# State-space rounds of a hybrid encoder block: carried products in five PSUM places, transposes in three, and the first round's transposes and updates inside its last two projections

## The chip, the core and the metric

The kernel runs on one core of a Trainium2 chip. TensorE (PE in the profile) multiplies matrices and writes PSUM, VectorE (DVE) and ScalarE (ACT) read PSUM and work on SBUF, GpSimd (POOL) works on SBUF alone, and SyncE (SP) issues the loads of the weights. PSUM has eight banks, each of 512 fp32 numbers a partition. The metric is the device time of one execution in microseconds; smaller is better.

## What is computed

One encoder block (feed-forward, mixer, feed-forward, norm) runs over 16 meta tokens, a prompt of 256 and a sample of 512 tokens, 784 columns together, with a width of 1024. The mixer has two branches; the change is in the first one, a bidirectional state-space scan (SSD) with 16 heads in 4 groups of 4. It is computed in chunks of 128 tokens: two of the prompt, four of the sample. The reference does this for each direction:

```python
def ssd_chunked(x, dt, A, Bm, Cm):
    ...
    CB = jnp.einsum('bctgn,bcsgn->bctsg', Cc, Bc)
    y_diag = jnp.einsum('bctsg,bctsgh,bcsghp->bctghp', CB, Lm, xdt)
    decay_to_end = jnp.exp(acs[:, :, -1:] - acs)
    states = jnp.einsum('bcsgn,bcsgh,bcsghp->bcghpn', Bc, decay_to_end, xdt)
    chunk_decay = jnp.exp(acs[:, :, -1])

    def step(h, inp):
        st, dec = inp
        return dec[..., None, None] * h + st, h
    ...
    y_off = jnp.einsum('bctgn,bcghpn,bctgh->bctghp', Cc, prev, jnp.exp(acs))
    return (y_diag + y_off).reshape(b, T, H, P)
```

## The kernel before

**Projections.** Every weight is split into a high part `whi` (ScalarE) and a low part `wlo` (in this stage by VectorE, helper `low`, L1844), and a projection of 128 output columns is a `job`: for each of 8 slices `t` of the width six matmuls (three products, two column halves) that add up in one of two PSUM slots, `slot[0]` and `slot[1]`, of two banks each. This is a `t` step; a job has 48 matmuls, all on L514. The other four banks are `aux[0]` to `aux[3]`, which the profile names by the tile `aux`.

**A round.** There are four rounds, one for each group of heads (`GROUPS`). A round has six jobs: 0 and 1 for x, 2 for B, 3 for C, 4 and 5 for the gate z. For jobs 0 to 3 ScalarE copies the slot to `ci` (`ssd_read`), VectorE convolves it (`convolve`, L1915 and L1917) and ScalarE applies SiLU and writes `co` (L1249, semaphore `co_ok`). Around the jobs, TensorE does this for the round:

- `ssd_turn`, L738: 8 groups of three transposes (two groups of 16 meta tokens, then the six chunks) into `aux[n % 2]`. ScalarE copies each to `xbt` (L1274, `tr_ok`). Group n waits for the copy of group n - 2.
- `ssd_updates`, L753: ten products for the chunks' states. GpSimd makes the operands `xw` first (L2331), six of them in `co`; VectorE copies the results to `prev` or adds them to the decayed state before (L1940, L1944, L1946, semaphore `up_ok`).
- `ssd_carried`: six products of C and B (L765, `CB` of the reference, in `aux[2]` and `aux[3]`), once all states are there, and then for each chunk c the product of C and the carried state (L774, `y_off` of the reference) into `aux[c % 2]`, 256 columns for each of one or two directions. VectorE multiplies each by its decay and writes it to `prev` (L1953, `off_ok`). Chunk c waits for VectorE to be done with chunk c - 2.
- `ssd_step(k)`, five times: decay products (L791), exponentials (ScalarE, L1290) and outputs (L801, L804), whose gates VectorE applies (`gates`, L1989).

The trace shows each fp32 matmul of L753, L765 and L774 as two entries, so ten instructions of L774 are 20 entries. A transpose is one entry.

**Order.** Every engine has its instructions in an order written out by hand, and waits for semaphores in it; nothing is scheduled at run time. The first round stands ahead of a loop (`Fori`) of three passes. Each pass has jobs 1 to 5 of the next group N between steps 0 to 4 of the group G, then updates and carried products of N, then job 0 of the group behind it. On VectorE a pass has at its end `ssd_updates(N)`, `weighted(G)` (L2003 to L2011), `decays(0, N)` (L1978), one `low`, and `ssd_carried(N)`. In the first round it is `ssd_updates`, `decays(0)`, `low`, `ssd_carried`. GpSimd's products `xdt` (L2339) follow its `xw`.

Ahead of the loop TensorE has this, with the job ahead of `ssd_carried` finished before the first update begins:

```python
            pe.wait_ge(dt_all, 1)
            ssd_turn(first)
            ssd_job(5, first)
            ssd_updates(first)
            ssd_carried(first)
            ssd_job(0, (1, None))
```

## Time and profile before

| | us |
|---|---|
| median of 3 runs | 2342.83 (2342.05 to 2344.07) |
| the profiled execution | 2344.32 |
| its span in the trace | 2342.8 |
| TensorE busy with matmuls | 2263.5 (97%) |
| VectorE busy | 1445.8 (62%) |
| ScalarE busy | 1025.9 (44%) |
| GpSimd busy | 365.4 (16%) |

The profile shows one execution. A busy TensorE there means that a matmul is in flight; a wait shows as idle time in square brackets, with the instruction that ended it. TensorE's clock has two levels, 1.2 and 2.4 GHz; a granted clock of 1.00 is the upper one, 0.50 the lower. The state-space rounds lie between 593 and 977 us: the first round to 660, the three passes of the loop from there to about 747, 833 and 918.

### The profile page before, as it was taken

What the parts mean: (1) busy time and instruction counts of PE and PEld (TensorE: products, weight loads), DVE (VectorE), ACT (ScalarE), POOL (GpSimd) and SP (SyncE); (2) the same over time, 40 slices, a digit from 0 to 9 for tenths busy, and PEclk for the clock granted to TensorE, in tenths of its full rate; (3) what the DMA queues carried; (4) which work ended last, traced back from release to release, by engine and by line L of the source; (5) the groups of instructions that cost most, each with busy time, mean ns of one, the idle gap of its engine ahead of it and who ended that gap; (6) DMA issues with size and microseconds to landing.
All of it is one profiled execution on the core that took longest, in us unless ns stands there. A gap on an engine that the chain in (4) does not pass through costs nothing.

```text
span 2342.8 us, 36390 instructions
## 1 busy us (share of the span) xinstructions
PE 2263.5 (97%) x13148; PEld 2017.3 (86%) x13148; DVE 1445.8 (62%) x2345; ACT 1025.9 (44%) x1659; POOL 365.4 (16%) x256
## 2 busy tenths in 40 slices
PE   8999999998999999999999999999999999999997
PEld 7899999997877777888888888888888899899996
DVE  7667677677788888413444444442237667677677
ACT  6334243244464664523555566644125333243344
POOL 2000000000101201134323333322333100000000
PEclk9999999998999999999999999999999999999998
DMA  3221221223111111132111111111332132221211
GB/s 118 65 73 55 72 72 54 72 57 105 46 37 37 36 36 39 52 97 75 46 37 45 45 45 45 36 37 46 103 121 74 56 86 56 66 78 54 72 54 72
DMA packets 252273, 144.65 MB, mean 62 GB/s; under 512 B 5712, under 2 KB 248576, under 8 KB 252176
## 3 DMA queue, kind: packets, MB, share of 16 engines
q1 hardware_dynamic: 249072, 130.63, 20.0%
q0 software_dynamic: 2336, 12.58, 1.5%
q8 instruction: 62, 1.02, 0.2%
q14 instruction: 35, 0.29, 0.0%
q10 hardware_dynamic: 768, 0.13, 0.0%
HBM read 133.89 MB, written 9.44 MB: 61 GB/s over the span
## 4 chain that ended last, share of the span: by engine, by line
PE 78%; DVE 8%; issue 7%; ACT 5%; POOL 1%; DMA 0%; ACTq 0%; DVEq 0%; POOLq 0%
PE slot L514 31%; PE aux L545 23%; PE slot L594 14%; PE aux L913 2%; PE aux L804 1%; POOL wlo L2269 1%; PE aux L791 1%; PE aux L881 1%; PE aux L906 1%; PE aux L894 1%; PE slot L681 1%; ACT whi L985 1%; PE aux L774 1%; DVE ca L1917 1%; DVE hprev L2163 0%
## 5 line engine op out<-in xcount | busy, mean ns | idle before, releaser
L2269 POOL TENSOR_TENSOR wlo<-raw,whi 128x1024 fp32r<-128x1024 f32 (+1 forms) x100 | 227.0, 2270 | 1061.1 <-ACT whi L985 1061.0
L514 PE MATMUL slot<-xh,whi 128*128 128x256 f32 (+1 forms) x1360 | 361.5, 347 | 5.5 <-DVE gate L1575 2.3
L514 PE MATMUL slot<-xh,wlo 128*128 128x256 f32 (+1 forms) x1360 | 351.7, 340 | 0.0
L514 PE MATMUL slot<-xl,whi 128*128 128x256 f32 (+1 forms) x1360 | 350.8, 340 | 0.0
L514 PEld LDWEIGHTS slot<-xh,whi 128*128 128x128 f32 x1360 | 252.7, 188 | 43.2 <-issue 9.7
L514 PEld LDWEIGHTS slot<-xh,wlo 128*128 128x128 f32 x1360 | 256.0, 188 | 30.1
L514 PEld LDWEIGHTS slot<-xl,whi 128*128 128x128 f32 x1360 | 256.2, 189 | 29.8
L545 PE MATMUL aux<-th,whi 128*128 128x392 f32 (+1 forms) x640 | 220.8, 345 | 9.1 <-ACT work L1089 5.2
L1063 ACT ACTIVATE whi<-work 128x512 fp32r<-128x512 f32 x220 | 135.6, 626 | 198.5 <-DVE work L1633 105.1
L545 PE MATMUL aux<-tl,whi 128*128 128x392 f32 (+1 forms) x640 | 216.6, 338 | 0.0
L545 PE MATMUL aux<-th,wlo 128*128 128x392 f32 (+1 forms) x640 | 215.9, 337 | 0.0
L1612 DVE TENSOR_TENSOR wlo<-work,whi 128x512 fp32r<-128x512 f32 x220 | 151.4, 689 | 80.0 <-ACT whi L1063 79.9
L985 ACT ACTIVATE whi<-raw 128x1024 fp32r<-128x1024 f32 (+1 forms) x129 | 125.5, 973 | 102.6 <-PE slot L514 85.4
L545 PE MATMUL aux<-xh,whi 128*128 128x392 f32 (+1 forms) x480 | 163.0, 340 | 2.4 <-DVE prod L1685 2.4
L545 PE MATMUL aux<-xl,whi 128*128 128x392 f32 (+1 forms) x480 | 162.8, 339 | 0.0
L545 PE MATMUL aux<-xh,wlo 128*128 128x392 f32 (+1 forms) x480 | 162.1, 338 | 0.0
L594 PE MATMUL slot<-ah,whi 128*128 128x272 f32 (+1 forms) x608 | 159.1, 343 | 1.1 <-DVE al L1654 0.4
L594 PE MATMUL slot<-al,whi 128*128 128x272 f32 (+1 forms) x608 | 156.9, 340 | 0.0
L594 PE MATMUL slot<-ah,wlo 128*128 128x272 f32 (+1 forms) x608 | 156.9, 340 | 0.0
L545 PEld LDWEIGHTS aux<-th,whi 128*128 128x128 f32 x640 | 120.1, 188 | 20.4 <-issue 10.7
L1703 DVE SCALAR_TENSOR_TENSOR gate<-slot,rs 128x784 f32<-128x784 f32 (+1 forms) x76 | 73.4, 966 | 102.1 <-PE slot L594 102.0
L594 PEld LDWEIGHTS slot<-ah,whi 128*128 128x128 f32 x608 | 113.4, 188 | 16.6 <-issue 3.4
(339 smaller groups left out, 4361.4 us busy)
## 6 DMA issues: line engine op xcount, KB each, us to landing
raw<-in_w_in SPq DMA_DIRECT2D x81, 512.0 KB, 3.9
raw<-in_ffn_w_gate_up SPq DMA_DIRECT2D x48, 512.0 KB, 4.4
work<-in_ffn_w_gate_up SPq DMA_DIRECT2D x40, 512.0 KB, 4.6
raw<-in_ffn_w_down SPq DMA_DIRECT2D x80, 256.0 KB, 3.0
raw<-in_ssd_w_proj SPq DMA_DIRECT2D x8, 512.0 KB, 4.0
raw<-in_hg_w_proj SPq DMA_DIRECT2D x8, 512.0 KB, 3.8
raw<-in_w_out SPq DMA_DIRECT2D x8, 512.0 KB, 3.8
h_spill<-h POOLq DMA_DIRECT2D x1, 3072.0 KB, 10.9
```

The lines of the kernel that those rows point to most:

```text
L514: mm = pe.matmul(slot[b][:, PC + u:PC + v], w[b][:, t, :], x[:, t, u + off:v + off], start=(t == 0 and p == 0 and q == 0), stop=(t == k - ...
L545: mm = pe.matmul(aux[bank][:, 0:NT - mid], w[:, t, :], x, start=(first and t == 0 and n == 0), stop=(t == HK - 1 and n == 2), skip_group_c ...
L594: mm = pe.matmul(slot[d % 2][:, PC + u:PC + e], quarter(w, v)[:, t, :], x[:, t, u:e], start=(t == 0 and n == 0), stop=(t == PAIRS - 1 and ...
L681: return pe.matmul(slot[j % 2][:, PC + u:PC + v], w[j % 2][:, t, :], x[:, t, u:v], start=first, stop=last)
L774: mm = pe.matmul(aux[c % 2][:, 2 * P * d:2 * P * (d + 1)], m_s["co"][3][:, t:t + P], m_s["prev"][d][:, c, :], start=True, stop=True)
L791: mm = pe.matmul(aux[u % 3][:, :], strict[d][:, :], v[u % 3][:, :, :], start=(p == 0), stop=(p == 1))
L913: mm = pe.matmul(out[:, 64 * u:64 * u + 64], m_h["prev"][d][:, c, :], m_h["q"][d][0][:, t:t + 64], start=False, stop=True, skip_group_chec ...
L985: act.activation(whi[s % 2][:, 0:k, :], raw[s % 2][:, 0:k, :], ACT.Copy).then_inc(w_hi, 1)
L1063: act.activation(quarter(whi, v), operand(m_, n % 2), ACT.Copy).then_inc(q_hi, 1)
L1612: dve.tensor_tensor(quarter(wlo, v), operand(m_, n % 2), quarter(whi, v).bitcast(F32), sub).then_inc(q_lo, 1)
L1703: dve.scalar_tensor_tensor(m["t"][:, c0:], slot[b][:, PC + c0:], 0.5, rs[:, c0:], mul, mul).then_inc(dn_free[b], 1)
L2269: pool.tensor_tensor(wlo[s % 2][:, 0:k, :], raw[s % 2][:, 0:k, :], whi[s % 2][:, 0:k, :].bitcast(F32), ALU.subtract).then_inc(w_lo, 1)
```

## The change

`ssd_turn` uses three banks, `aux[n % 3]`, on TensorE and on ScalarE, and takes a range of groups; group n waits for the copy of group n - 3. The carried products have places of their own (`CARRY`, `carry_bank`): chunks 0 and 1 in the two banks of the slot in which job 0 of the next round will stand, chunks 2 and 3 in `aux[0]` and `aux[1]`, chunk 5 (one direction) in the free half of `aux[3]`. Chunk 4 takes `aux[0]` once more, and its product is moved behind the first `t` step of that next job 0. `ssd_carried` begins by waiting for the slot, and ends by waiting until VectorE has read chunks 0 and 1. In the first round the transposes stand by pairs of groups ahead of `t` steps 4 to 7 of job 4, the updates ahead of `t` step 5 of job 5; the wait for `dt_all` moves ahead of job 4, and VectorE's `low` of the next round's job 0 moves ahead of its `ssd_updates`. ScalarE's order stays.

```diff
+        CARRY = [0, 1, 2, 3, 5, 4]
+
+        def carry_bank(c):
+
+            b = slot[(J_SSD + 6) % 2]
+            return {0: b[:, 0:BANK], 1: b[:, BANK:], 2: aux[0], 3: aux[1], 4: aux[0], 5: aux[3][:, 2 * P:]}[c]
...
                     for t in range(k):
+                        if t in between:
+                            between[t]()
                         if ready:
...
-            def ssd_turn(G):
+            def ssd_turn(G, first=0, last=NC + 2):
 
                 wait(pe, co_ok, 4, 3, G)
-                for n in range(NC + 2):
+                for n in range(first, last):
                     k, t = (N_META, CO_META[n]) if n < 2 else (P, CO_CHUNK[n - 2])
-                    if n >= 2:
-                        wait(pe, tr_ok, NC + 2, n - 1, G)
+                    if n >= 3:
+                        wait(pe, tr_ok, NC + 2, n - 2, G)
                     else:
                         wait(pe, exp_ok, 2 * NC, n - 2, G)
                     for q in range(3):
-                        mm = pe.transpose(aux[n % 2][0:k, P * q:P * (q + 1)], m_s["co"][q][:, t:t + k], ident[:, :])
+                        mm = pe.transpose(aux[n % 3][0:k, P * q:P * (q + 1)], m_s["co"][q][:, t:t + k], ident[:, :])
                     mm.then_inc(tr_mm, 1)
...
                 mm.then_inc(cb_mm, 1)
-                for c in range(NC):
-                    if c >= 2:
-                        wait(pe, off_ok, NC, c - 1, G)
-                    t = CO_CHUNK[c]
-                    for d in range(2):
-                        if not (d == 1 and c in (CP - 1, NC - 1)):
-                            mm = pe.matmul(aux[c % 2][:, 2 * P * d:2 * P * (d + 1)], m_s["co"][3][:, t:t + P], m_s["prev"][d][:, c, :],
-                                           start=True, stop=True)
-                    mm.then_inc(off_mm, 1)
+                s = J_SSD + 6 * (G[0] + 1)
+                pe.wait_ge(slot_free[s % 2], lin(s // 2, 3, G[1]))
+                for n in range(NC - 1):
+                    carried_chunk(n, G)
+                wait(pe, off_ok, NC, 2, G)
+
+            def carried_chunk(n, G):
+
+                c = CARRY[n]
+                t, bank = CO_CHUNK[c], carry_bank(c)
+                if n == NC - 1:
+                    wait(pe, off_ok, NC, CARRY.index(2) + 1, G)
+                for d in range(2):
+                    if not (d == 1 and c in (CP - 1, NC - 1)):
+                        mm = pe.matmul(bank[:, 2 * P * d:2 * P * (d + 1)], m_s["co"][3][:, t:t + P], m_s["prev"][d][:, c, :],
+                                       start=True, stop=True)
+                mm.then_inc(off_mm, 1)
...
             first = (0, None)
-            for c in range(5):
-                if c:
-                    ssd_job(c, first)
-                if c == 0:
-                    dt_turn()
-                if c == 2:
-                    dt_part()
+            dt_turn()
+            ssd_job(1, first)
+            ssd_job(2, first)
+            dt_part()
+            ssd_job(3, first)
             pe.wait_ge(dt_all, 1)
-            ssd_turn(first)
-            ssd_job(5, first)
-            ssd_updates(first)
+            ssd_job(4, first, {t: lambda t=t: ssd_turn(first, 2 * t - 8, 2 * t - 6) for t in range(4, KT)})
+            ssd_job(5, first, {5: lambda: ssd_updates(first)})
             ssd_carried(first)
-            ssd_job(0, (1, None))
+            ssd_job(0, (1, None), {1: lambda: carried_chunk(NC - 1, first)})
...
-                ssd_job(0, (2, g))
+                ssd_job(0, (2, g), {1: lambda: carried_chunk(NC - 1, N)})
...
             def ssd_carried(G):
-                for c in range(NC):
-                    wait(dve, off_mm, NC, c + 1, G)
+                for n, c in enumerate(CARRY):
+                    wait(dve, off_mm, NC, n + 1, G)
...
             convolve(3, first)
+            low(J_SSD + 6, 0, None)
             ssd_updates(first)
             decays(0, first)
-            low(J_SSD + 6, 0, None)
             ssd_carried(first)
```

The order of the instructions at three places follows. L523, L747, L762, L774 and L791 of the changed kernel are L514, L738, L753, L765 and L774 of the one before.

TensorE, first round, end of job 4 and start of job 5 (before):

```order
L514 MATMUL slot<-xh,wlo 128x256
L514 MATMUL slot<-xh,wlo 128x512
L738 MATMUL aux<-ident,co 16x128 x6
L738 MATMUL aux<-ident,co 128x128 x18
L514 MATMUL slot<-xh,whi 128x256
```

The same in the changed kernel, from the end of `t` step 3 of job 4:

```order
L523 MATMUL slot<-xh,wlo 128x256
L523 MATMUL slot<-xh,wlo 128x512
L747 MATMUL aux<-ident,co 16x128 x6
L523 MATMUL slot<-xh,whi 128x256
L523 MATMUL slot<-xh,whi 128x512
L523 MATMUL slot<-xl,whi 128x256
L523 MATMUL slot<-xl,whi 128x512
L523 MATMUL slot<-xh,wlo 128x256
L523 MATMUL slot<-xh,wlo 128x512
L747 MATMUL aux<-ident,co 128x128 x6
L523 MATMUL slot<-xh,whi 128x256
```

The 24 transposes stood behind the job; now six stand between two `t` steps each.

TensorE, first round, from the end of job 5 to job 0 of the next round (before):

```order
L514 MATMUL slot<-xh,wlo 128x512
L753 MATMUL aux<-xw,xbt 128x256 x4
L753 MATMUL aux<-co,xbt 128x256 x6
L765 MATMUL aux<-co 128x128 x6
L774 MATMUL aux<-prev,co 128x256 x10
L514 MATMUL slot<-xh,whi 128x272
L514 MATMUL slot<-xh,whi 128x512
```

The same in the changed kernel, from the end of `t` step 4 of job 5:

```order
L523 MATMUL slot<-xh,wlo 128x512
L762 MATMUL aux<-xw,xbt 128x256 x4
L762 MATMUL aux<-co,xbt 128x256 x6
L523 MATMUL slot<-xh,whi 128x256
...
L523 MATMUL slot<-xh,wlo 128x512
L774 MATMUL aux<-co 128x128 x6
L791 MATMUL slot<-prev,co 128x256 x3
L791 MATMUL aux<-prev,co 128x256 x5
...
L523 MATMUL slot<-xh,wlo 128x272
L523 MATMUL slot<-xh,wlo 128x512
L791 MATMUL aux<-prev,co 128x256 x2
L523 MATMUL slot<-xh,whi 128x272
```

The updates moved three `t` steps up, three of the ten carried products write the slot, and the last two stand inside the next job.

VectorE, first round, from the `low` of job 5 to the carried products (before):

```order
L1844 TENSOR_TENSOR wlo<-raw,whi 128x1024
L1915 TENSOR_SCALAR ca<-ci,gw 128x802
L1917 SCALAR_TENSOR_TENSOR ca<-ci,gw,ca 128x802 x4
L1940 COPY prev<-aux 128x256 x4
L1944 TENSOR_TENSOR prev<-prev,gcd 128x256
...
L1946 TENSOR_TENSOR prev<-prev,aux 128x256
L1978 TENSOR_TENSOR rh<-incl,gah 128x512 x3
L1844 TENSOR_TENSOR wlo<-raw,whi 128x1024
L1953 TENSOR_TENSOR prev<-aux,gec 128x256 x10
```

The same in the changed kernel:

```order
L1858 TENSOR_TENSOR wlo<-raw,whi 128x1024
L1929 TENSOR_SCALAR ca<-ci,gw 128x802
L1931 SCALAR_TENSOR_TENSOR ca<-ci,gw,ca 128x802 x4
L1858 TENSOR_TENSOR wlo<-raw,whi 128x1024
L1954 COPY prev<-aux 128x256 x4
L1958 TENSOR_TENSOR prev<-prev,gcd 128x256
...
L1960 TENSOR_TENSOR prev<-prev,aux 128x256
L1992 TENSOR_TENSOR rh<-incl,gah 128x512 x3
L1967 TENSOR_TENSOR prev<-slot,gec 128x256 x3
L1967 TENSOR_TENSOR prev<-aux,gec 128x256 x7
```

The second `low` moved from behind `rh` to ahead of the updates' copies.

## Rows read from the trace of the kernel before

**Rows 1.** The page, part 4: shares of the chain that ended last.

```profile
PE 78%; DVE 8%; issue 7%; ACT 5%; POOL 1%; DMA 0%; ACTq 0%; DVEq 0%; POOLq 0%
```

**Rows 2.** TensorE's waits, 585 to 985 us: total, times, longest.

```profile
PE aux L774 <- DVE prev L1953: 7.2, 4, 2.2
PE aux L765 <- DVE prev L1946: 3.7, 1, 3.7
PE aux L738 <- ACT xbt L1274: 2.9, 12, 0.3
```

**Rows 3.** TensorE in order of time, first round: start, length (us), line, operation, count.

```profile
632.32 0.82 PE L738 MATMUL aux<-ident,co 128*16 128x128 f32 x6
...
636.32 0.60 PE L514 MATMUL slot<-xh,whi 128*128 128x256 f32 x2
...
644.90 2.19 PE L753 MATMUL aux<-xw,xbt 16*128 16x256 f32 x8
...
653.42 1.60 PE L765 MATMUL aux<-co 128*128 128x128 f32 x12 [3.74 <-DVE prev L1946]
...
657.03 3.54 PE L774 MATMUL aux<-prev,co 128*128 128x256 f32 x14 [0.70 <-DVE prev L1953]
660.22 0.70 PE L514 MATMUL slot<-xh,whi 128*128 128x272 f32 x2
```

**Rows 4.** All engines in order of time, first round.

```profile
627.49 0.97 ACT L1249 ACTIVATE co<-ca,gw 128x802 f32<-128x802 f32 x1 [1.42 <-DVE ca L1917]
...
637.74 3.47 POOL L2331 TENSOR_TENSOR co<-xbt,gw_t 128x256 f32<-128x256 f32 x6
...
638.53 1.06 ACT L985 ACTIVATE whi<-raw 128x1024 fp32r<-128x1024 f32 x1
...
641.17 2.33 POOL L2339 TENSOR_TENSOR xdt<-xbt,gdt 128x256 f32<-128x256 f32 x4
...
646.06 0.76 DVE L1940 COPY prev<-aux 128x256 f32<-128x256 f32 x2 [12.51 <-PE aux L753]
...
653.28 1.89 DVE L1978 TENSOR_TENSOR rh<-incl,gah 128x512 fp32r<-128x512 f32 x3
...
655.09 1.22 DVE L1844 TENSOR_TENSOR wlo<-raw,whi 128x1024 fp32r<-128x1024 f32 x1
```

**Rows 5.** TensorE in order of time, last pass of the loop.

```profile
911.54 1.46 PE L774 MATMUL aux<-prev,co 128*128 128x256 f32 x6
915.16 3.54 PE L774 MATMUL aux<-prev,co 128*128 128x256 f32 x14 [2.16 <-DVE prev L1953]
918.36 0.70 PE L514 MATMUL slot<-xh,whi 128*128 128x272 f32 x2
```

**Rows 6.** VectorE in order of time, last pass of the loop.

```profile
854.77 0.49 DVE L1989 TENSOR_TENSOR work<-aux,work 128x128 f32<-128x128 f32 x2 [2.29 <-PE aux L804]
...
889.79 8.08 DVE L1844 TENSOR_TENSOR wlo<-raw,whi 128x1024 fp32r<-128x1024 f32 x1
898.36 0.76 DVE L1940 COPY prev<-aux 128x256 f32<-128x256 f32 x2 [0.48 <-PE aux L753]
899.42 0.75 DVE L1940 COPY prev<-aux 128x256 f32<-128x256 f32 x2 [0.30 <-PE aux L753]
...
914.36 1.08 DVE L1953 TENSOR_TENSOR prev<-aux,gec 128x256 f32<-128x256 f32 x3
```

**Rows 7.** TensorE in order of time, transposes of the last pass.

```profile
880.51 0.49 PE L738 MATMUL aux<-ident,co 128*16 128x128 f32 x3
...
884.44 0.93 PE L738 MATMUL aux<-ident,co 128*128 128x128 f32 x6 [0.20 <-ACT xbt L1274]
885.21 0.27 PE L801 MATMUL aux<-ident,prev 128*128 128x128 f32 x1
```

**Rows 8.** TensorE in order of time, first pass of the loop.

```profile
742.57 4.98 PE L774 MATMUL aux<-prev,co 128*128 128x256 f32 x14 [2.17 <-DVE prev L1953]
```

**Rows 9.** Busy time by stretch; the last three columns: clock, DMA share, GB/s.

```profile
742.50:747.20 4.70, 4.63 (x15) 3.74 (x15) 2.06 (x7) 0.56 (x2) 0.00 (x0) 0.64 0.43 112
```

10 lines of the change are left out of this document (5 added, 5 removed).

## The prediction, made before the changed kernel had run

> **What bounds the kernel now.** I read the chain that ended last first: three quarters of it is TensorE [rows 1]. So a microsecond is worth something only where TensorE stands still, or where VectorE reaches a point earlier that TensorE waits for later. Next I read TensorE's waits in the state-space rounds. Three kinds matter: the carried products L774 wait for VectorE's reads (7.2 us in four waits), the products ahead of them wait once for the last state of the first round (3.7 us), and the transposes L738 wait for ScalarE's copies (2.9 us in twelve, three in each round) [rows 2]. That is 13.8 us, an upper bound for what goes by waits alone. Then I read both engines in order of time around each wait, to see who is late next.
>
> **First round, transposes.** They take from 632.32 to 636.32, 4.00 us [rows 3]. Without waits, the 6 narrow ones start (0.82 - 0.27) / 5 = 0.11 us apart [rows 3, 7], the 18 wide ones (0.93 - 0.27) / 5 = 0.13 us [rows 7]: 0.66 + 2.34 = 3.0 us. Inside job 4 each pair of groups is followed by a `t` step of 8.58 / 8 = 1.07 us (job 5: 636.32 to 644.90 [rows 3]), which covers ScalarE's two copies. But the first pair now stands at 632.32 - 4 x 1.07 = 628.0, and the `co` of job 2 is written only at 627.49 + 0.97 = 628.46 [rows 4]: a new wait of 0.4 us, with the other half of job 4 queued behind it. Each return to a projection costs about 0.1 us (the first two matmuls behind a foreign block take 0.60 or 0.70 us [rows 3]; at the job's own spacing they would take about 0.5); there are four, so 0.4. New total 3.8, a gain of 0.2 us. Bounds: -0.5 (each return 0.2 and a longer `co` wait) and 1.0 (nothing but the 3.0).
>
> **First round, updates.** From the start of the updates to the products L765 it is 644.90 to 653.42, 8.52 us, of which 3.74 are idle [rows 3]. VectorE sets this: it begins at 646.06, after an idle time of 12.51 us, and ends as it turns to `rh` at 653.28 [rows 4]. If the chain of updates keeps its length, three `t` steps (3 x 1.07 = 3.2 us) lie inside those 8.52 us. One more return costs 0.1. Gain 3.1; some 0.5 us of waiting are left. VectorE must be free in time. Its `low`, moved ahead of the updates, needs the high part that ScalarE writes after job 4. Job 4 ends at about 636.1, and ScalarE then reads the slot and writes the high part, which alone takes 1.06 us [rows 4]; for both I estimate twice that, so it is there at about 638.3, in the middle of GpSimd's products, which end some 1.6 us earlier than before: they ran from 637.74 to 641.17 + 2.33 = 643.5 [rows 4]. The updates start at about 636.1 + 5 x 1.07 = 641.5, so VectorE is wanted at 642.5, and the operands (done by about 640) are ready. In the loop a `low` beside the same chain of GpSimd took 8.08 us [rows 6]; in the first round, with GpSimd at rest, it took 1.22 [rows 4]. So VectorE can come free as late as 643.3, 0.8 us late. Bounds of this term: 2.3 and 3.2. I take 3.1, because in the loop GpSimd had just begun, and here it is in its last third.
>
> The Trainium skill (SBUF — State Buffer, "SBUF: two separate sides") says that VectorE with two inputs in SBUF and GpSimd share a pair of ports under an exclusive lock, which the one that starts first holds for its whole instruction. By that rule a `low` waits for one GpSimd product and is hidden; the 8.08 us in the loop show a wait over many [rows 6], which is the lower bound above, so the trace speaks for the harsher case.
>
> **First round, carried products.** From L765 to the next job it is 653.42 to 660.22, 6.80 us [rows 3]. L765 takes 1.4 of it (1.60 less the tail of its last entry). The carried entries start at most 3.19 / 14 = 0.23 us apart, with a wait among them (657.03 to 660.22) [rows 3]; I take 0.22. Now 16 of 20 stand ahead of the job: 3.5 us. VectorE, busy with `rh` for 1.8 us after the last state [rows 4], has read chunks 0 and 1 before those 4.9 us are over: its first product is there after 1.4 + 0.9, and three reads take 1.1 [rows 6]. So 1.9 us are gained before the job, and chunk 4 inside it costs 4 x 0.22 = 0.9 plus 0.1 for the return: 0.9 us net. First round in all: 0.2 + 3.1 + 0.9 = 4.2 us.
>
> **Each pass of the loop, carried products.** Here VectorE comes late, after `weighted`, `rh` and a `low`. It starts reading at 914.36; TensorE gets its first release at 915.16 and starts the job at 918.36, 4.00 us after VectorE's start [rows 5, 6]. With places for all, TensorE's own work is over at 911.54 + 16 x 0.22 = 915.1, and it needs VectorE's first three reads: 914.36 + 1.08 + 0.06 = 915.5 [rows 5, 6]. The wait of 2.16 us becomes one of 0.4, and the job starts 2.85 us earlier. Chunk 4 in it costs 1.0. Gain 1.85 us for TensorE. Its wait inside the job costs nothing: VectorE reads chunk 2 by 916.3, the product is due at 915.5 + 1.07 = 916.6. Bounds 1.2 (chunk 4's wait bites for 0.6) and 2.2.
>
> Does VectorE keep up? It loses its own waits between the reads, and it has 2.29 us of idle time ahead of the first gates of the next pass [rows 6]. It waits for TensorE there, so from that point on it is earlier by all that TensorE has gained.
>
> **Each pass, transposes.** 880.51 to 885.21, 4.70 us [rows 7]. A third bank takes away the waits for the copies, about 0.25 each [rows 2] and a little refill: 0.8 us, but not ScalarE's own pace of some 0.45 us a copy. For TensorE alone this is worth nothing, since VectorE decides at the pass's end. But VectorE waits 0.48 and 0.30 us for the first two pairs of updates [rows 6]; with TensorE 0.8 us earlier both go. VectorE's `low` of 8.08 us stays as it is, as GpSimd starts relative to VectorE as before. Gain 0.8 us, bounds 0 and 0.9.
>
> A pass: 1.85 + 0.8 = 2.65 us. Three passes: 8.0 us.
>
> **The clock.** In the first pass the 14 entries behind the wait take 4.98 us; in the others they take 3.54 [rows 5, 8]. The granted clock of that stretch is 0.64 [rows 9], so 1.4 us there are from a stretch at the lower level, after 2.17 us of idleness. With idle times of half a microsecond I expect none: 1.4 us more. Similar stretches stand in the later stages, which the change only moves in time; each one more or less is 1.4 us either way, and I allow for two.
>
> **The sum.** 4.2 + 8.0 + 1.4 = 13.6 us. The profiled execution took 2344.32 us, which gives 2330.7; from the median of 2342.83 it gives 2329.2. I forecast 2329.5. With all bounds at their worst (first round 2.3, a pass 1.2, the clock 0) it is 5.9 us and about 2337; at their best (first round 5.4, a pass 3.1, the clock 1.4 and 2.8 from later stages) 18.9 us, about 2324.
>
> **Rivals.**
> 1. *VectorE becomes the bound inside a pass.* It would then earn only its own waits: in the carried reads and ahead of the updates, 0.78 us there [rows 6] and as much again between the reads by my estimate, 1.5 us a pass. 4.2 + 4.5 + 1.4 = 10.1 us, 2332.7. For it: VectorE is the releaser of nearly every wait in these rounds [rows 2]. Against it: the 2.29 us in which it waits [rows 6]. Chance 0.12.
> 2. *Only the loop gains.* The fixed order in the first round only exchanges one wait for another: `co` ahead of the transposes, a starved `low` ahead of the updates, and the state chain is not moved. 8.0 + 1.4 = 9.4 us, 2333.4. Against it: VectorE's idle 12.51 us [rows 4]. Chance 0.07.
> 3. *The change does not do what it says.* The wait for the two reads of the slot takes the place of the old one, because VectorE itself gets later (it reads without pauses only if the products are there). Then the loop gains 0.5 us a pass at most: 4.2 + 1.5 = 5.7 us, 2337.1. Chance 0.05.
> 4. *Slower.* The places where small fp32 products now interrupt a projection lower the clock. There are nine (five in jobs 4 and 5, four in the jobs 0). If each brought a stretch like that of rows 9, it would cost 4.70 x (1 - 0.64) = 1.7 us [rows 9], in all 15.3 us, against a gain of 12.2 us without the clock term: 3 us slower, 2346. It decides the sign from eight such places on. Against it: the transposes and updates in their present places follow dense jobs too, and their spacing shows the upper level [rows 3, 7]. Chance 0.03.
>
> **How the numbers follow.** The forecast has 0.73; its own range is 2326.5 to 2332.5. The range given, 2325.5 to 2334.0, reaches over rivals 1 and 2 and leaves out 3, 4 and the outermost clock cases. A measurement of this kernel can tell 0.2%, 4.7 us, from no change: faster means below 2338.1. The forecast, rivals 1 and 2 and most of 3 lie there: 0.93. Within 0.2% lie the rest of rival 3 and part of rival 4: 0.05. Slower, rival 4 with more or longer stretches: 0.02.
>
> **What would show it.** In the first round: a wait of 0.4 us for `co` ahead of the first transposes, and half a microsecond or a little more ahead of L765's counterpart in place of 3.74. In each pass: a wait of about 0.4 us at the end of the carried products or the start of job 0, none between them, 0.8 us less in the transposes, and a distance from pass to pass that falls by 2.65 from (915.16 - 742.57 - 1.4) / 2 = 85.6 us [rows 5, 8] to 82.9. No stretch at the lower clock between 640 and 910. The prediction is wrong if VectorE's waits ahead of L1989's counterpart vanish (rival 1), or if the `low` of the first round ends after 643.

## The result, and the profile of the changed kernel

| | before | changed |
|---|---|---|
| median | 2342.72 us (2341.43 to 2344.45, 6 runs) | 2323.73 us (2321.93 to 2330.6, 6 runs) |
| the profiled execution, its span | 2344.32, 2342.8 | 2324.22, 2322.7 |

The ratio is 0.9923 (0.9911 to 0.9936): 19 us less, where 13.3 were forecast and 17.3 were the most that the range allowed. Each kernel's time varies from one execution to the next by up to 12 us (2334.78 to 2346.35 before, over all comparisons). In the profiles the number and the place of the stretches at TensorE's lower clock vary with it; medians, the fastest executions and the intervals between marks in the traces are therefore read side by side below.

Numbers of lines in the changed kernel: jobs L523, transposes L747, updates L762, products of C and B L774, carried products L791, decay products L808, outputs L818 and L821; on VectorE `low` L1858, updates L1954 to L1960, reads of carried products L1967, `rh` L1992, gates L2003, `weighted` L2017 to L2025.

The page of the changed kernel, part 4. The shares answer to [rows 1]:

```profile
PE 74%; DVE 12%; issue 7%; ACT 5%; POOL 1%; ACTq 0%; DVEq 0%; DMA 0%; POOLq 0%
```

TensorE's waits, 585 to 985 us, changed kernel (in all, times, longest, us). They answer to [rows 2]:

```profile
PE slot L523 <- DVE wlo L1858: 3.6, 5, 1.4
PE slot L523 <- DVE prev L1967: 2.0, 3, 0.7
PE aux L747 <- ACT e L1304: 1.0, 3, 0.3
PE aux L808 <- DVE rh L1992: 0.7, 3, 0.2
PE aux L774 <- DVE prev L1960: 0.6, 1, 0.6
```

The three kinds of [rows 2], 13.8 us, are gone or small. Two waits are new in each pass: one of 0.65 us ahead of job 0, for the reads (foreseen as 0.4), and one of 0.52 us ahead of job 1, for its low part (three of the five in the first line; not foreseen).

TensorE in order of time, changed kernel, first round (start, length, line, operation, count; in brackets the idle time ahead of it and what ended it). It answers to [rows 3]:

```profile
627.79 0.82 PE L747 MATMUL aux<-ident,co 128*16 128x128 f32 x6 [0.25 <-ACT co L1263]
628.37 0.59 PE L523 MATMUL slot<-xh,whi 128*128 128x256 f32 x2
...
634.61 0.51 PE L523 MATMUL slot<-xh,whi 128*128 128x256 f32 x2
...
648.49 1.60 PE L774 MATMUL aux<-co 128*128 128x128 f32 x12 [0.60 <-DVE prev L1960]
...
653.20 0.71 PE L523 MATMUL slot<-xh,whi 128*128 128x272 f32 x2
```

The same, first pass of the loop, from the transposes to job 1. It answers to [rows 5, 7]:

```profile
702.52 0.50 PE L747 MATMUL aux<-ident,co 128*16 128x128 f32 x3
703.36 2.93 PE L747 MATMUL aux<-ident,co 128*16 128x128 f32 x21 [0.34 <-ACT e L1304]
706.12 0.27 PE L818 MATMUL aux<-ident,prev 128*128 128x128 f32 x1
...
736.72 0.59 PE L523 MATMUL slot<-xh,whi 128*128 128x272 f32 x2 [0.65 <-DVE prev L1967]
...
746.23 0.40 PE L808 MATMUL aux<-rh,strict 128*128 128x512 f32 x1
...
748.31 0.61 PE L523 MATMUL slot<-xh,whi 128*128 128x272 f32 x2 [0.52 <-DVE wlo L1858]
```

And of the kernel before, the part of its second pass that the rows above leave out:

```profile
832.78 0.71 PE L514 MATMUL slot<-xh,whi 128*128 128x272 f32 x2
...
841.54 0.40 PE L791 MATMUL aux<-rh,strict 128*128 128x512 f32 x1
...
842.93 0.51 PE L514 MATMUL slot<-xh,whi 128*128 128x272 f32 x2
```

**Where the 20.1 us of the span went.** I laid marks on both traces: the first transposes of dt (593.82 and 593.11), step 0 of each round (its first decay product), and the first norm sum of the HGRN heads (1165.67 and 1151.94), the stage behind.

| stretch | before | changed | gain |
|---|---|---|---|
| up to the dt transposes | 593.82 | 593.11 | 0.7 |
| from there to step 0 of the first round | 75.16 | 69.71 | 5.45 |
| step 0 to step 0, second and third pass | 85.58, 85.58 | 83.45, 83.45 | 2.13 each |
| the same, first pass | 86.98 | 83.41 | 3.57, of which 1.44 are the clock |
| from step 0 of the last round to the first norm sum | 238.55 | 238.81 | -0.26 |
| all of it, from the dt transposes to the first norm sum | 571.85 | 558.83 | 13.0 |
| from the first norm sum to the end | 1177.1 | 1170.8 | 6.4 |

So the part of the span that the change touches gave 13.0 us, against a forecast of 13.6. The rest lies in stages whose code the change leaves alone. The 0.7 us ahead of the first mark go with the clock too: from 560 us to that mark the mean granted clock is 0.80 before and 0.85 in the changed kernel. The 6.4 us lie in the heads. The eight HGRN heads follow each other there, and each of the first five head steps, from one norm sum to the next, has one of two lengths. Busy time by stretch, kernel before, head steps 1, 5, 6 and 7 (columns: length, busy time of PE, PEld, DVE, ACT and POOL, then clock, DMA share, GB/s):

```profile
1165.67:1230.51 64.84, 62.91 (x399) 55.48 (x398) 30.12 (x65) 36.09 (x42) 20.74 (x10) 0.97 0.17 42
1425.06:1489.93 64.87, 62.94 (x400) 55.52 (x398) 30.14 (x65) 36.08 (x42) 20.73 (x10) 0.97 0.16 40
1489.93:1553.04 63.11, 61.27 (x400) 53.90 (x399) 30.28 (x65) 34.80 (x41) 20.64 (x10) 1.00 0.16 42
1553.04:1600.78 47.74, 44.28 (x303) 38.97 (x302) 19.00 (x52) 26.15 (x31) 15.44 (x8) 1.00 0.18 45
```

The same of the changed kernel, head steps 1, 5 and 6:

```profile
1151.94:1215.16 63.22, 61.29 (x400) 53.85 (x399) 30.15 (x65) 36.09 (x42) 20.82 (x10) 1.00 0.17 43
1404.81:1469.69 64.88, 62.95 (x399) 55.51 (x398) 30.17 (x65) 36.09 (x42) 20.81 (x10) 0.97 0.16 40
1469.69:1532.83 63.14, 61.30 (x399) 53.90 (x398) 30.27 (x65) 34.82 (x41) 20.63 (x10) 1.00 0.16 42
```

A "long" head step has a mean clock of 0.97 and takes 64.85 us, a short one has 1.00 and takes 63.22: 1.63 us for one stretch at the lower level. All of the first five are long before, one is in the changed kernel, and 4 x 1.63 = 6.5 us accounts for the 6.4 of this stage. The sixth step is short in every profile. The seventh has no next job beside it and takes 47.75 us; in five of the fifteen profiles it holds a stretch of its own and takes 1.1 or 3.0 us more, which the count of long steps doesn't show.

### The profile page after: what moved, and what is told of

It reads as the page before. It is cut to its first block, busy times and chain, and to the rows that moved or that the text cites. A ratio compares the mean times of both kernels' runs of the same rounds, so it can differ in the third digit from the quotient of the medians.

```text
span 2322.7 us, 36388 instructions
## 1 busy us (share of the span) xinstructions
PE 2253.0 (97%) x13148; PEld 2008.7 (86%) x13148; DVE 1445.7 (62%) x2345; ACT 1025.9 (44%) x1659; POOL 367.8 (16%) x256
## 4 chain that ended last, share of the span: by engine, by line
PE 74%; DVE 12%; issue 7%; ACT 5%; POOL 1%; ACTq 0%; DVEq 0%; DMA 0%; POOLq 0%
PE slot L523 29%; PE aux L554 23%; PE slot L603 14%; DVE ca L1931 1%; PE aux L927 1%; DVE wlo L1858 1%; POOL wlo L2283 1%; PE aux L895 1%; PE aux L821 1%; PE aux L808 1%; PE aux L920 1%; PE aux L908 1%; PE slot L690 1%; ACT whi L999 1%; DVE hprev L2177 0%
## 5 line engine op out<-in xcount | busy, mean ns | idle before, releaser
L523 PE MATMUL slot<-xh,whi 128*128 128x256 f32 (+1 forms) x1360 | 362.4, 348 | 9.0 <-DVE wlo L1858 3.6
L523 PE MATMUL slot<-xh,wlo 128*128 128x256 f32 (+1 forms) x1360 | 351.8, 340 | 0.0
L523 PE MATMUL slot<-xl,whi 128*128 128x256 f32 (+1 forms) x1360 | 350.6, 340 | 0.0
L523 PEld LDWEIGHTS slot<-xh,whi 128*128 128x128 f32 x1360 | 251.9, 188 | 49.0 <-issue 15.6
L523 PEld LDWEIGHTS slot<-xh,wlo 128*128 128x128 f32 x1360 | 256.1, 188 | 30.1
L523 PEld LDWEIGHTS slot<-xl,whi 128*128 128x128 f32 x1360 | 255.9, 189 | 29.8
```

Of the source, the lines that this page charges most:

```text
L523: mm = pe.matmul(slot[b][:, PC + u:PC + v], w[b][:, t, :], x[:, t, u + off:v + off], start=(t == 0 and p == 0 and q == 0), stop=(t == k - ...
```

## Experiments

### One part of the change at a time

`only_banks`: the kernel before with three banks for the transposes, and nothing else.

```diff
-                    if n >= 2:
-                        wait(pe, tr_ok, NC + 2, n - 1, G)
+                    if n >= 3:
+                        wait(pe, tr_ok, NC + 2, n - 2, G)
...
-                        mm = pe.transpose(aux[n % 2][0:k, ...
+                        mm = pe.transpose(aux[n % 3][0:k, ...
```

> The kernel before with the transposes in three banks, nothing else. Place of reading: the first product of the heads' norm sums, at 1165.67 us in the kernel before and 1151.94 in the changed one; it lies behind all the rounds and ahead of the stretches at the lower clock in the heads. Theory (the prediction's): each pass of the loop turns 0.8 us less of transposes into 0.8 us through VectorE's waits for the updates, so 2.4 us in three passes and 0.3 in the first round: 1163.0. Rival: ScalarE's copies set the pace or VectorE's next wait takes it back, so at most 0.2 a pass: 1165.0.

`only_places`: the kernel before with `CARRY`, `carry_bank` and `carried_chunk` of the change, in the first round and in the loop.

```diff
-            ssd_job(0, (1, None))
+            ssd_job(0, (1, None), {1: lambda: carried_chunk(NC - 1, first)})
...
-                ssd_job(0, (2, g))
+                ssd_job(0, (2, g), {1: lambda: carried_chunk(NC - 1, N)})
```

> The kernel before with the places of the carried products, chunk 4 inside the next job, nothing else. Theory: 1.85 us a pass less 0.5 for a new wait for the low part of job 1, so 1.3 to 1.4, plus 0.9 in the first round and 1.4 for the stretch at the lower clock at 744 us: 6.4 us, the heads' first norm sum at 1159.3. Rival (VectorE is the bound inside a pass and the transposes' third bank is needed for the rest): under 3.5 us, 1162.2 or later.

`only_first`: the kernel before with the moved transposes, updates and `low` of the first round.

```diff
-            ssd_turn(first)
-            ssd_job(5, first)
-            ssd_updates(first)
+            ssd_job(4, first, {t: lambda t=t: ssd_turn(first, 2 * t - 8, 2 * t - 6) for t in range(4, KT)})
+            ssd_job(5, first, {5: lambda: ssd_updates(first)})
...
+            low(J_SSD + 6, 0, None)
             ssd_updates(first)
             decays(0, first)
-            low(J_SSD + 6, 0, None)
```

> The kernel before with the first round's moves alone (transposes inside job 4, updates inside job 5, VectorE's low part of the next job ahead of the updates). Theory: 0.2 + 3.1 = 3.3 us by the prediction; the trace of the changed kernel shows the start of the first products behind the last state at 648.49 against 653.42, less 0.7 us that was there before the rounds began, so 4.2 us. Read there and at the heads' first norm sum: 1161.5. Rival: the low part, moved, costs what the updates gain, 1 to 2 us in all, 1164.

| | median us (range, runs) | ratio | to step 0, first round | a pass | heads' first norm sum, expected |
|---|---|---|---|---|---|
| before | 2342.0 (2334.95 to 2346.35, 31) | | 75.16 | 85.58 | 1165.67 |
| three banks | 2337.45 (2331.48 to 2341.05, 10) | 0.9985 (0.9972 to 0.9998) | | 84.59 | 1164.71, 1163.0 |
| carried places | 2334.41 (2329.23 to 2340.3, 10) | 0.9974 (0.9958 to 0.9989) | | 84.43 | 1160.15, 1159.3 |
| first round | 2330.52 (2329.88 to 2335.45, 10) | 0.9963 (0.9951 to 0.9975) | 70.66 | 85.55 | 1159.45, 1161.5 |

(Of the first two a stretch at the lower clock falls into the first round, so its length is left out; with the banks alone the first two passes have one too, and the third is given.) The norm sum misses its expected place by 0.9 to 2.1 us each time; such stretches, which come and go, are part of it, so I read the intervals without one. The banks are worth 0.99 us a pass, the places 1.15, together 2.14: the whole change's 2.13. They add up, so neither hides the other. The moves of the first round are worth 4.50 of its 5.45 us. The medians vary by more than these parts, as the number of long head steps does: 5 in the profile of before, 1 with the places alone, none with the banks or the first round alone. Nine of the ten executions of the first round's moves lie within 1.8 us (2329.88 to 2331.65), 11 us below the median of before, where its rounds account for 6.

The run with the first round's moves leaves the loop as it was, with its wait of 2.17 us at the end of the first pass, and yet the products behind that wait take 3.54 us, not the 4.98 of [rows 8]:

```profile
737.79 3.54 PE L776 MATMUL aux<-prev,co 128*128 128x256 f32 x14 [2.17 <-DVE prev L1952]
```

So the wait does not bring the stretch in every execution.

TensorE's waits with the carried places alone show where job 1's wait comes from (585 to 985 us):

```profile
PE slot L523 <- DVE wlo L1861: 3.7, 5, 1.4
PE aux L747 <- ACT xbt L1291: 2.9, 12, 0.3
PE slot L523 <- DVE prev L1970: 1.6, 3, 0.6
```

### Does the place in time of the heads decide their clock?

`before_d8` and `after_d4` put 16 and 8 throwaway matmuls (2.84 and 1.42 us) ahead of the first head's projections, in the kernel before and in the changed one; the head's own matmuls overwrite their results.

```diff
+            low_ready(pe, J_HG)
+            pe.wait_ge(slot_free[J_HG % 2], J_HG // 2)
+            for _ in range(8):
+                for u, v in halves(0):
+                    pe.matmul(slot[J_HG % 2][:, PC + u:PC + v], whi[J_HG % 2][:, 0, :], xh[:, 0, u:v], start=True, stop=True)
```

> The kernel before with eight extra pairs of matmuls (2.84 us of TensorE work, results overwritten) ahead of the first job of the heads. It tests the 6.5 us that the prediction missed: in the heads five of seven have a stretch at the lower clock in the kernel before, one has in the changed kernel, and a head with one is 64.85 us long against 63.2. Theory A (whether a head's pause falls into such a stretch depends only on when it comes, and one such stretch brings the next head to the same place again): moved by 2.84 us the heads lie nearly as in the changed kernel, at most one or two stretches are left, and the kernel is faster than the one before by 3 to 6 us although it does more work: about 2338. Theory B (the changed kernel's earlier stages have something to do with it, as in a warmer chip or other transfers): five stretches stay, 2345.6.

Measured: 2342.15 us (2339.7 to 2343.68, 10 runs), ratio 1.0009 (0.9998 to 1.0019). None of the first five head steps of its profile is long (63.20 to 63.24), but the stretches at the lower clock stand elsewhere in it: one in the first round, whose way to step 0 takes 77.02 us, and one in the seventh head step, which takes 50.77 us in place of 47.75. The first pass has none (85.52 us), though its code and its wait of 2.17 us are those of before. The 2338 of theory A is missed, and so are the five long steps and the 2345.6 of theory B.

> The changed kernel itself, again, beside the kernel before on another chip. In the last comparison the kernel before took from 2334.95 to 2346.35 us, as many as its stretches at the lower clock in the heads say (1.74 us each). Theory A (the rounds give a fixed gain of 13.0 us, and the rest of the 19 us is how many heads had such a stretch in those executions): the fastest runs of both lie 13.0 to 13.5 us apart, 2321.5 against 2335; the medians lie between 11 and 20 us apart, and the changed kernel spreads to 2328 or more now and then. Theory B (the changed kernel has fewer stretches in every execution, by its place in time): all but a few of its runs under 2325, medians 18 us or more apart.

> The changed kernel with four extra pairs of matmuls (1.42 us of TensorE work, results overwritten) ahead of the first job of the heads. If the place in time of the heads decides how many stretches at the lower clock there are (theory B), the median moves by something else than 1.42 us: by 5 us or more up if the new place is a bad one, and the profile shows three or more long heads of 64.85 us. If it is chance in each execution (theory A), the median and the fastest run move by 1.4 us and the spread stays.

Measured: `after_same`, the changed kernel again, 2323.81 us (2322.89 to 2327.45, 4 runs), ratio 0.9932 (0.9904 to 0.9959); `after_d4` 2327.52 us (2323.74 to 2331.8, 6 runs), 0.9943. The interval of the rounds is 558.93 in the one (558.83 in the first profile of the same kernel) and 560.33 in the other, 1.4 more, as built. But the profile of `after_same` has three long head steps and that of `after_d4` five. The first profile of the changed kernel had one. Neither theory is settled by this: the fastest executions lie 11.9 us apart (2322.89 and 2334.81), where theory A of `after_same` wanted 13.0 to 13.5, and the delay moved the median by 3.7 us and the fastest execution by 0.85, where the two theories of `after_d4` wanted 1.4 or at least 5. So the same kernel differs from execution to execution, and one profile doesn't tell a kernel's number.

### Do the pauses in the heads cause it?

In each head TensorE stands still twice for about half a microsecond between short products. TensorE in order of time, kernel before, first head:

```profile
1208.71 0.49 PE L881 MATMUL aux<-vt,kt 64*128 64x128 f32 x2 [0.49 <-DVE hprev L2163]
1209.23 0.71 PE L894 MATMUL aux<-q 128*128 128x128 f32 x4
1210.52 0.71 PE L894 MATMUL aux<-q 128*128 128x128 f32 x4 [0.58 <-DVE hprev L2163]
1211.07 0.84 PE L906 MATMUL aux<-am,vt 128*128 128x128 f32 x4
1211.70 1.81 PE L913 MATMUL aux<-q,hprev 128*128 128x64 f32 x8
```

The changed kernel has the same pauses, without the stretch behind them:

```profile
1194.97 0.48 PE L895 MATMUL aux<-vt,kt 64*128 64x128 f32 x2 [0.49 <-DVE hprev L2177]
1195.48 0.71 PE L908 MATMUL aux<-q 128*128 128x128 f32 x4
1196.77 0.71 PE L908 MATMUL aux<-q 128*128 128x128 f32 x4 [0.58 <-DVE hprev L2177]
1197.32 0.63 PE L920 MATMUL aux<-am,vt 128*128 128x128 f32 x4
1197.79 1.00 PE L927 MATMUL aux<-q,hprev 128*128 128x64 f32 x8
```

Eight products of the last line take 1.81 us in the one and 1.00 in the other. In every long head step of the eight profiles that have any, the clock falls to its lower level once, and every time this begins 0.7 to 0.9 us behind the end of the pause of 0.58 us. `before_fill` and `after_fill` put two throwaway matmuls (a slice of the next job, overwritten by that job) into each of the two pauses, in every head but the last.

```diff
+            def hg_fill(j, i, count):
...
+                        pe.matmul(slot[s % 2][:, PC + u:PC + v], whi[s % 2][:, 0, :], xh[:, 0, u:v], start=True, stop=True)
...
+                    if u == len(H_BANKS) - 1 and j < HH - 1:
+                        hg_fill(j, i, 1)
...
+                if j < HH - 1:
+                    hg_fill(j, i, 1)
```

> The changed kernel with one extra pair of dense matmuls in each of the two places in a head where TensorE waits about half a microsecond for VectorE (ahead of the last states and ahead of the second chunk's products), 14 pairs of 0.36 us in all, results overwritten. Theory: these two pauses bring the stretches at the lower clock; the pairs fit into the waits but for some 0.1 us each, so each head is 63.2 to 63.5 us long, none is 64.85, and the runs spread by no more than 3 us around 2322 to 2324. Rival (the small products around the pauses bring them, not the pauses): long heads stay, and the median rises by up to 2 us over the changed kernel's.

> The kernel before with the dense pair of matmuls in each of the two pauses of a head (14 pairs, results overwritten). In the kernel before, most executions take 2340 to 2345 us, with four or five long heads, and the fastest 2335, with none by theory. Theory (the pauses of half a microsecond bring the stretches at the lower clock): no long head, the median falls to 2335 to 2337.5 although the kernel does more work, and the spread falls to about 3 us. Rival (chance, or the small products themselves): long heads as before, the median at 2342 or more.

Measured: `after_fill` 2325.3 us (2322.21 to 2327.03, 5 runs), ratio 0.9934, the first five head steps 63.20 to 63.23; `before_fill` 2335.97 us (2335.29 to 2340.52, 7 runs), beside 2342.52 of before (2334.82 to 2344.61, 17 runs), ratio 0.9981 (0.9967 to 0.9994). Head steps 1 and 5 of `before_fill`, both short, and then the seventh of `after_fill`:

```profile
1164.57:1227.81 63.24, 62.16 (x404) 54.38 (x403) 30.15 (x65) 36.08 (x42) 20.77 (x10) 1.00 0.17 43
1417.44:1480.69 63.25, 62.16 (x404) 54.40 (x403) 30.16 (x65) 36.08 (x42) 20.78 (x10) 1.00 0.17 41
```

```profile
1531.45:1580.29 48.84, 45.76 (x303) 40.32 (x302) 19.11 (x52) 26.16 (x31) 15.45 (x8) 0.97 0.17 44
```

The kernel before gets 6.5 us faster at the median by doing more work: the four matmuls of a head (404 entries in place of 399 or 400) fill its first pause and leave 0.23 us of the second, and the long steps go. Six of its seven executions lie between 2335.3 and 2336.9, close to the fastest of before. The fill costs a head step nothing (63.24 us against 63.23 for a short one without it). What is left in both profiles is one stretch in the last head, the only one whose pauses are not filled (48.84 us in place of 47.75).

This agrees with the theory that the pauses bring the stretches, and the place of the stretches speaks for it, but it does not leave chance out altogether. Four of the twelve profiles without a fill have no long head step either, and `only_first` has nearly all its executions close together with the pauses as they were. On the changed kernel the fill was worth nothing that the runs show: the median is 1.5 us above that of `after_same`, and the executions spread over 4.8 us, where at most 3 were expected.

### What bounds a pass now?

`both`: in the changed kernel the low part of job 1 is made ahead of the read of chunk 4, and `rh` behind the reads.

```diff
+                    if n == NC - 1:
+                        early()
...
-                decays(0, N)
-                ssd_carried(N)
+                ssd_carried(N, lambda: low(J_SSD + 6 + 7, 6, g))
...
+                decays(0, G)
```

> The changed kernel with two more moves on VectorE in every round: the low part of job 1 of the next round ahead of the read of chunk 4's carried product (VectorE waits 0.8 us there, TensorE waits 0.52 us for this low part later), and the decay operands rh behind the carried reads instead of ahead of them (TensorE waits 0.65 us for the first reads at each pass's end). Theory: both waits go, so a pass takes 83.45 - 1.17 = 82.3 us, and 3 to 4 us are gained in all. Rival (VectorE has no time left in a pass: its chain from the reads to the masks of step 0 gets longer and TensorE waits there instead): a pass of 83.0 or more.

Measured: 2322.8 us (2322.48 to 2329.33, 4 runs), ratio 0.9928, a pass 83.18 to 83.23, 0.25 less, where the theory had 82.3. The rival holds: both waits went, and one for VectorE's mask products came (L1988), ahead of decay products. It is in this list, 585 to 985 us:

```profile
PE aux L808 <- DVE prev L1988: 4.5, 4, 1.2
```

`low_first`: in the changed kernel the `low` that took 8.08 us [rows 6] stands ahead of the scan vectors that GpSimd's products wait for. `weighted_early`: the same, and `weighted` ahead of the updates.

```diff
+                low(J_SSD + 6 + 5, 6, g)
                 scan_vectors(N)
-                low(J_SSD + 6 + 5, 6, g)
...
-                ssd_updates(N)
                 weighted(G)
+                ssd_updates(N)
```

(The last three lines are those of `weighted_early` alone.)

> The changed kernel with VectorE's low part of job 5 moved ahead of the copies that release GpSimd (scan_vectors) in each pass. Theory: the 8.08 us that this subtraction takes in each pass are a wait behind GpSimd's chain of products; issued ahead of it, it takes 1.2 to 1.5 us. TensorE's updates set VectorE's start then, 0.5 us earlier than now, so 0.3 to 0.5 us a pass: 83.0 to 83.2 in place of 83.45. Rival (the 8.08 us have another cause, such as a wait that the profile doesn't show, or a later operation takes over the stall): one VectorE operation in that place still takes over 5 us, and the pass stays at 83.4 or gets longer.

> As low_first, and with the squares and weights of the finished group (weighted, 5.5 us of VectorE) ahead of the updates instead of behind them, in the time that the stalled subtraction took. Theory: they fit between 713 and 719 us beside GpSimd, slowed by up to a quarter; VectorE reaches the carried products 5 us earlier, so both waits of TensorE there go (0.65 and 0.52 us a pass): 82.3 us a pass, 3.4 us in all, about 2320. Rival (each of these operations has two inputs in SBUF too and waits behind GpSimd's chain as the subtraction did): VectorE comes late to the updates instead, and a pass takes 83.4 us or more.

VectorE in order of time, `low_first`:

```profile
710.14 1.22 DVE L1858 TENSOR_TENSOR wlo<-raw,whi 128x1024 fp32r<-128x1024 f32 x1
...
719.09 0.76 DVE L1954 COPY prev<-aux 128x256 f32<-128x256 f32 x2 [6.24 <-PE aux L762]
```

VectorE and then GpSimd, `weighted_early`:

```profile
711.73 0.87 DVE L2003 TENSOR_TENSOR work<-aux,work 128x128 f32<-128x128 f32 x4
712.52 7.02 DVE L2017 COPY gn<-vec_b 128x2 f32 x1
719.58 1.33 DVE L2020 TENSOR_TENSOR rs<-work 128x768 f32<-128x768 f32 x1
```

```profile
712.06 2.32 POOL L2345 TENSOR_TENSOR xw<-xbt,gw_t 16x256 f32<-16x256 f32 x4 [8.15 <-DVE gw_t L1945]
714.34 3.46 POOL L2345 TENSOR_TENSOR co<-xbt,gw_t 128x256 f32<-128x256 f32 x6
717.77 2.31 POOL L2353 TENSOR_TENSOR xdt<-xbt,gdt 128x256 f32<-128x256 f32 x4
```

Measured: `low_first` 2322.21 us (2321.19 to 2328.53, 4 runs), ratio 0.9912 (0.9896 to 0.9927), a pass 83.30 to 83.34, a little above the 83.0 to 83.2 of the theory: the `low` falls from 8.08 to 1.22 us, and VectorE then waits 6.24 us for TensorE's updates. `weighted_early` 2343.5 us (2342.07 to 2346.04, 11 runs), 1.0013: a copy of two numbers a partition takes 7.02 us. It ends at 719.54, when GpSimd is in its last products, `weighted` and the updates come behind it, TensorE waits up to 4.6 us for them, and a pass takes 88.8 us. The stall is not a property of `low`; in these two kernels it hits VectorE's next operation between SBUF tiles that falls beside GpSimd's chain.

The Trainium skill (SBUF — State Buffer, "SBUF: two separate sides") has an exclusive lock on a port pair, held for one instruction, for GpSimd and for VectorE with two inputs in SBUF or in a faster copy mode. That VectorE stands still altogether, and that a small copy between SBUF tiles is caught too, agrees with the 7.02 and 8.08 us. That the wait ends with the running instruction does not: no GpSimd product in that window takes over 0.61 us (3.46 us for six), and the copy spans twelve of them from start to end. In the first round of the changed kernel it is otherwise: there the `low` took 1.53 us beside the same kind of chain, and GpSimd's six products beside it took 4.46 us in place of 3.47. What makes the difference no run here tells.

### Taken together, and the changed kernel once more

`rh_between`: the changed kernel with `low_first`, with `rh` between the reads of chunks 5 and 4, and with the fills of the heads. `after_more` is the changed kernel itself.

```diff
                 for n, c in enumerate(CARRY):
+                    if n == NC - 1:
+                        decays(0, G)
```

> The changed kernel with three further moves. The low part of job 5's states is made ahead of the scan vectors (as in low_first, where it took 1.22 us and the pass came to 83.30 to 83.34 us). The vector rh of a step is made between the read of chunk 5 and the read of chunk 4, where both behind the reads was worth 83.18 to 83.21 us a pass with a new wait of 1.18 us on the mask products. And two throwaway matmuls stand in the two pauses of each head step, as in after_fill, whose head steps were all 63.2 us at no cost. Their results are overwritten. Theory A (what is left in a pass is the wait of 0.65 us of job 0 for the reads and 0.52 us of job 1 for its low part; the heads' 1.7 us each come from their pauses): pass 82.9 to 83.1 us, three passes 1.0 to 1.5 us under the changed kernel, no head step of 64.85 us, median 2320.5 to 2321.5. Rival B (the end of a pass is bound by all of VectorE's work there, so that a move only renames the wait): pass 83.2 to 83.45, median 2322 to 2323.5, still without long head steps.

> The changed kernel itself, again, beside the kernel before. Open is whether its small number of head steps of 64.85 us comes from where its heads now lie in time or by chance. Theory A (each execution draws its number of low-clock stretches, and the draw of the changed kernel is the lower one since its heads lie elsewhere): median 2322.5 to 2324.5 again, with one run in five or so at 2327 to 2331, and the kernel before at 2342 with one run in four near 2335. Rival B (chance of the first runs alone): the runs of the changed kernel spread like those of before, over 8 to 10 us with the median near 2329 (2322 of the fastest and 4 head steps of 1.7 us).

Measured, beside before with 2343.31 us (2334.78 to 2344.11, 11 runs): `rh_between` 2324.47 (2321.83 to 2326.44, 6 runs), ratio 0.9924 (0.9912 to 0.9937); `after_more` 2327.82 (2321.53 to 2332.48, 6 runs), 0.9933 (0.9915 to 0.9952). A pass of `rh_between` takes 82.94 to 83.00 us as its first theory said, and no head step is long. TensorE's waits for it, 585 to 985 us:

```profile
PE slot L523 <- DVE wlo L1871: 4.8, 6, 1.4
```

The wait for the reads is gone, and job 1's for its low part is there still, now 0.78 us in the first pass. Of the 1.4 us that the passes gain, 0.4 go again behind the last one: the rounds take 557.91 us, 0.92 less than in the changed kernel. The median missed its 2320.5 to 2321.5; executions up to 2326.44 may have stretches elsewhere, but none of those was profiled. Whether it beats the changed kernel the intervals don't tell.

`after_more` answers the question on chance partly. Its median misses the 2322.5 to 2324.5 of theory A and lies nearer the 2329 of rival B. The first five head steps of its profile are all long, and there is one more stretch ahead of the first norm sum. All 16 executions of the changed kernel together: 11 lie below 2325, one is at 2327.45, four lie between 2330.6 and 2332.5. Of 75 executions of before, 16 lie below 2337, the others between 2338.5 and 2346.35. Within 3.5 us of their own fastest (2321.53 and 2334.78) lie 11 of the 16, and of the kernel before 16 of 75. So the two kernels do seem to draw differently, and the first six executions of the changed kernel were neither all luck nor a fixed gain.

## Why the forecast was too small

**The rounds, 13.6 forecast, 13.0 measured.** The mechanisms are the forecast ones, several terms are not, and that the sums agree so well is in part luck: the first round gave 5.45 us where 4.2 were forecast, the three passes 6.4 where 8.0 were, the clock 1.44 where 1.4 were, and 0.26 were lost behind the last pass.

- *First round, transposes: 0.2 forecast, 1.0 measured* (job 5 starts 42.50 us behind the dt transposes before, 41.50 changed). The step that failed is the spacing of 0.13 us "without waits" and the returns put on top of it. A pair of groups that stands by itself moves the next `t` step by 628.37 - 627.79 = 0.58 us. With their returns the four pairs cost 634.61 - 627.79 - 4 x 1.07 = 2.5 us, not 3.4. The wait for `co` came, 0.25 us instead of 0.4. By these two the gain would be 1.2; the 0.2 us that are missing were lost ahead of the first pair.
- *Updates: 3.1 forecast, 3.2 measured.* L774 starts 648.49 - 634.61 = 13.88 us behind job 5, before it was 653.42 - 636.32 = 17.10. What is left of the wait is 0.60. The `low` took 1.53 us and ended at 638.4; the worry that GpSimd would hold it until 643.3 did not come true.
- *Carried products, first round: 0.9 forecast, 1.2 measured.* 6.80 us became 653.20 - 648.49 = 4.71, so 2.1 came ahead of the job; chunk 4 inside it cost 0.86.
- *Transposes in a pass: 0.8 forecast, 1.1 for TensorE, 0.99 for the pass* [rows 7]: 4.70 became 706.12 - 702.52 = 3.60. VectorE's waits of 0.48 and 0.30 us ahead of the updates are gone, as said.
- *Carried products in a pass: 1.85 forecast, 1.15 measured.* From the end of the transposes to job 0 it was 918.36 - 885.21 = 33.15 us [rows 5, 7] and is 736.72 - 706.12 = 30.60: 2.55 us earlier, against 2.85. Chunk 4 cost 0.75, job 0 to step 0 being 9.51 in place of 8.76. And from step 0 to job 1 it is 2.08 in place of 1.39: 0.69 lost, which the forecast did not have. The step that failed is "Does VectorE keep up?". It set the 2.29 us of idle time ahead of the gates against VectorE's lateness. But the `low` of job 1 stands ahead of those gates, behind the masks, and TensorE needs it first. From the first operation behind its reads to the end of that `low` VectorE takes 8.46 us in both kernels (the masks start at 833.86 and 739.72, the `low` ends at 842.32 and 748.18), and before the change the `low` was ready only 0.6 us ahead of job 1. Those 0.6 were all that could be gained there for nothing. This is rival 1's mechanism, at a smaller price than its 1.15 us a pass. The sign that the prediction gave for it, that VectorE's wait ahead of the first gates vanishes, did not come: it is 2.42 us. The sign stood behind the instruction that decided.
- *The clock at 744 us: 1.4 forecast, 1.44 measured.* The stretch is gone, and so is the wait of 2.17 us [rows 8, 9], but the wait alone does not make the stretch: `before_d8` and `only_first` have the wait and no stretch behind it. Over all profiles it looks like this. Of the six without the whole change, five have one or more stretches between 640 and 910 us. Of the nine with it, only `weighted_early` has any, one in each pass, behind its waits of up to 4.6 us. So the change does make them rarer, but how many it saves differs from execution to execution, and the agreement of this term is in part luck. The other 11.6 of the 13.0 us do not hang on the clock.

VectorE in order of time, changed kernel, end of the first pass. From 734.27 to the end of its `low` at 748.18 it has no pause but the one for chunk 4's product:

```profile
734.27 1.22 DVE L1858 TENSOR_TENSOR wlo<-raw,whi 128x1024 fp32r<-128x1024 f32 x1
735.40 1.07 DVE L1967 TENSOR_TENSOR prev<-slot,gec 128x256 f32<-128x256 f32 x3
...
738.93 0.76 DVE L1967 TENSOR_TENSOR prev<-aux,gec 128x256 f32<-128x256 f32 x2 [0.80 <-PE aux L791]
739.72 1.29 DVE L1974 TENSOR_TENSOR prev<-prev 128x256 f32<-128x256 f32 x2
...
746.95 1.23 DVE L1858 TENSOR_TENSOR wlo<-raw,whi 128x1024 fp32r<-128x1024 f32 x1
...
760.25 0.49 DVE L2003 TENSOR_TENSOR work<-aux,work 128x128 f32<-128x128 f32 x2 [2.42 <-PE aux L821]
```

**The rest, none forecast, 6.4 to 7.1 us measured.** The step that failed stands under "The clock": similar stretches in the later stages, "each one more or less is 1.4 us either way, and I allow for two". The mechanism was named, the term was mis-sized in two ways. A stretch in a head costs 1.63 us, and they don't come one by one: in the eight profiles that have long head steps, every step from the first long one to the fifth is long. The number is 1 to 5, and so the term is up to 8 us. The profile of before stood at its upper end, five of five, and the five could have been read in it: a kernel at the top of such a range can mostly go down. Four or five such steps fewer than in the profile of before, taken from the forecast of 2329.5, give 2323.0 and 2321.4; a range down to there would have held the median.

What is shown: the 13.0 us by marks in three profiles of the changed kernel, two without a stretch between the marks (558.83, 558.93) and one with one (560.53), against 571.85 before, which has one; by the fastest executions, 2334.78 - 2321.53 = 13.25; and the 6.4 us behind them by the long head steps of the two profiles. What is likely and not shown is that the pauses bring the heads' stretches. What stays open is why the changed kernel draws few of them more often. The place in time was a theory, and neither delay gave what it asked for.

## What to carry to other kernels

Where a second engine is credited with a margin, list all its instructions up to the margin, and ask which of them the first engine waits for on the way; the margin that counts is that of the nearest one. When a part of the time comes from clock stretches that recur in every iteration of some later stage, read how many iterations have one before the change: that number times their price belongs into the range, on the side on which there is room. And a short pause between small products can be worth filling with useless work: two matmuls in each cost a head step nothing, and the median of the kernel before fell by 6.5 us; on the changed kernel nothing was gained by it.

## What the runs showed of the hardware that I had not expected

- Stretches at the lower clock begin 0.7 to 0.9 us behind the second of two pauses of 0.49 and 0.58 us between short products, in some executions, and not in others of the same kernel. The Trainium skill (TensorE: Matmul & The Clock Gate, "HAM oscillation — how this bites in real kernels") tells of a clock that falls again at each recurring wait. The trace agrees in part: where it falls, it falls again 64.85 us later, in the next head, and once begun this holds to the fifth head step in all eight profiles that have it; but the other seven profiles, four of them with the same pauses unfilled, have no long step.
- VectorE can stand for about seven microseconds behind a chain of short GpSimd products (8.08 us for a `low` of 1.22, 7.02 us for a copy of 128x2), and GpSimd pays about 1 us for it: its last four products took 3.30 us beside the `low` and 2.31 without.
- Transposes that stand in sixes between matmuls of another shape cost about 0.6 us a group of six, return included; 21 in a row took 2.93 us, 0.13 apart.
